# Third layer's attention projections as three rounded products each, with the weights split by ScalarE and VectorE

## The reference, cut to what matters

```
h = modulate(rms_norm_2(x, norm_gain[i, 0]), sh1, sc1)
y = swa_sink_attention(h, swa_w_in[j], swa_qk_gain[j], swa_sinks[j], swa_w_out[j], cos, sin)
x = x + g1 * y
h = modulate(rms_norm_2(x, norm_gain[i, 1]), sh2, sc2)
x = x + g2 * swiglu(h, ffn_w_gate[i], ffn_w_up[i], ffn_w_down[i])
```

## Time and profile before

| | us |
|---|---|
| median of 3 runs (lowest, highest) | 1933.69 (1932.38, 1936.08) |
| the profiled execution's own time | 1934.44 |
| its span | 1932.2 |
| TensorE busy | 1751.9 (91%) |
| VectorE busy | 1185.4 (61%) |
| ScalarE busy | 854.7 (44%) |
| GpSimd busy | 56.8 (3%) |
| mean granted clock of TensorE | 0.972 of full speed |

### The profile page before, as it was taken

The page is one execution under the profiler, slowest core; times in us unless marked ns, Lnnn a source line. Parts: engine busy times, 40 slices in busy tenths (PEclk is TensorE's granted clock), DMA queues, the critical chain, the costliest instruction groups (busy, mean ns, idle before and its releaser), DMA issues.

```text
span 1932.2 us, 32871 instructions
## 1 busy us (share of the span) xinstructions
PE 1751.9 (91%) x13662; PEld 1432.8 (74%) x13662; DVE 1185.4 (61%) x2062; ACT 854.7 (44%) x1531; POOL 56.8 (3%) x96
## 2 busy tenths in 40 slices
PE   7998877677677699999999899999999999999999
PEld 4897544344344489888888798887688888988888
DVE  1885211011010288898877898884888887787674
ACT  2565100000000257655545665643565554766553
POOL 0200000000000000100000000000000000000000
PEclk9999998998998999999999999999999999999999
DMA  9777999999999975678674278775268866334543
GB/s 403 293 281 288 400 428 429 428 429 427 428 428 429 426 306 216 243 286 311 254 283 149 88 283 326 278 275 199 88 262 301 309 248 252 132 132 175 179 160 143
DMA packets 42771, 550.31 MB, mean 285 GB/s; under 512 B 5536, under 2 KB 6048, under 8 KB 8352
## 3 DMA queue, kind: packets, MB, share of 16 engines
q1 hardware_dynamic: 35136, 452.13, 58.9%
q0 software_dynamic: 7520, 96.56, 13.1%
HBM read 547.53 MB, written 1.05 MB: 284 GB/s over the span
## 4 chain that ended last, share of the span: by engine, by line
PE 66%; DMA 23%; DVE 8%; ACT 3%; issue 1%; SPq 0%; ACTq 0%; DVEq 0%
PE bank L709 24%; DMA ada_ring<-in_moe_side 16%; PE bank L713 13%; PE bank L699 12%; DMA ring<-in_moe 3%; PE bank L1136 3%; PE bank L1033 2%; PE bank L684 2%; DMA ring<-in_v 1%; PE bank L1141 1%; DMA ada_ring<-in_ada_last 1%; DVE ring_parts L2514 1%; PE bank L1327 1%; PE bank L805 1%; PE bank L1190 1%
## 5 line engine op out<-in xcount | busy, mean ns | idle before, releaser
L713 PEld LDWEIGHTS bank<-acts,ring_parts 128*128 128x128 f32 x2120 | 299.1, 190 | 23.3
L713 PE MATMUL bank<-acts,ring_parts 128*128 128x256 f32 x2120 | 315.1, 282 | 0.0
L709 PE MATMUL bank<-acts,mixT_parts 128*128 128x512 f32 x1004 | 252.8, 392 | 0.0
L2445 DVE TENSOR_TENSOR mixT<-mixT,bank 128x128 f32<-128x128 f32 x32 | 9.2, 288 | 340.5 <-ACT mixT L1711 340.5
L699 PE MATMUL bank<-acts,ring_parts 128*128 128x256 f32 x728 | 204.9, 281 | 0.0
L709 PEld LDWEIGHTS bank<-acts,mixT_parts 128*128 128x128 f32 x1004 | 180.0, 189 | 31.8
L1502 ACT CAST mixT_parts<-ring 128x1024 fp32r<-128x1024 f32 (+1 forms) x140 | 139.7, 1001 | 82.2 <-PE bank L713 79.5
L709 PE MATMUL bank<-acts,xn_parts 128*128 128x512 f32 x640 | 160.3, 392 | 0.0
L699 PEld LDWEIGHTS bank<-acts,ring_parts 128*128 128x128 f32 x728 | 137.9, 189 | 0.0
L709 PEld LDWEIGHTS bank<-acts,xn_parts 128*128 128x128 f32 x640 | 115.1, 189 | 20.6
L2342 DVE CUSTOM_DVE_ANT_0 ada_ring<-ada_ring,c_row 128x1024 f32<-128x1024 f32 x108 | 127.0, 1220 | 0.0
(11 more groups left out here) (438 smaller groups left out, 3333.8 us busy)
## 6 DMA issues: line engine op xcount, KB each, us to landing
ring<-in_moe SPq DMA_DIRECT2D x48, 2048.0 KB, 27.2
ada_ring<-in_moe_side SPq DMA_DIRECT2D x48, 2048.0 KB, 25.9
ada_ring<-in_ada POOLq DMA_DIRECT2D x45, 2048.0 KB, 9.8
ring<-in_gu SPq DMA_DIRECT2D x44, 2048.0 KB, 8.8
ring<-in_down SPq DMA_DIRECT2D x32, 1408.0 KB, 6.3
ring<-in_qk SPq DMA_DIRECT2D x12, 2048.0 KB, 8.5
ring<-in_out SPq DMA_DIRECT2D x9, 2048.0 KB, 8.4
ring<-in_na SPq DMA_DIRECT2D x8, 2048.0 KB, 8.9
```

Of the source, the lines that this page charges most:

```text
L709: mm(dst[:, :], w, both(*x), start=start, stop=False)
L713: return mm(dst[:, 0:T], w, x[0], start=False, stop=stop)
```

## The change

Layer 2's key, value and query products become split products, and its normalised input is split as in the other layers.

- The four places that asked whether a layer is split no longer ask. `normalise_split` runs for layer 2, with the casts of the first two weight pieces ahead of the norm and the third within it; the weights of keys and values are three pieces (0, 1 keys, 2 values) of one chunk, with high halves in the `piece_hi` buffers.
- TensorE's `swa_keys` takes, for each k tile, both key products (six instructions), each k tile when its low half is there, and then the values, 3 x 8 products of 128 columns for each half of the tokens.
- Each of the eight query tiles is cast by ScalarE (`cast_query`) and subtracted by VectorE (`low_query`). There are two buffers for the high halves, the DFT constants and `gact1`. ScalarE casts tile 0 after the key squares, 1 and 2 within the first steps, and tile j + 2 at the end of its turn j. VectorE subtracts tile 0 first, tile 1 after the cosine part of the keys, and tile j + 1 at the end of its turn j. TensorE waits for the subtraction of tile j ahead of the first half of query j.
- Squares of keys and queries go to `four_sq` instead of `xsq`, which holds the high half of the input now.
- VectorE's wait for the end of the value product moves ahead of the norm of the keys, since `qn` holds a high half until then.
- The counts of the semaphores follow.

```
-                        wait_chunk(pe, n)
-                        w = chunk3(n, 3 * P)
-                        project(bank[0][:, 0:T], w, 0, hT, x0)
-                        project(bank[0][:, T:2 * T], w, P, hT).then_inc(sw["k_proj"], 1)
-                        rows(bank[1][:, 0:T].rearrange("p (t n) -> p t n", t=TT), w, 2 * P, P, hT).then_inc(used[n % RING], 1)
+                        for k in range(KT):
+                            pe.wait_ge(h_lo, split_norms(i, False) + k + 1)
+                            for f in range(2):
+                                if k == 0:
+                                    pe.wait_ge(attn_lo, piece_splits(i) + f + 1)
+                                m = split_product(bank[0][:, f * T:(f + 1) * T], (kv_hi[f][:, k, :], part["w_kv"](n, f)[:, k, :]),
+                                                  (part["xsq"][:, k, :], part["hT"][:, k, :]), k == 0 and f == 0, k == KT - 1, True)
+                        m.then_inc(sw["k_proj"], 1)
+                        pe.wait_ge(attn_lo, piece_splits(i) + 3)
+                        for t in range(TT):
+                            for k in range(KT):
+                                m = split_product(bank[1][:, t * P:(t + 1) * P], tuple(part[x][:, k, t * P:(t + 1) * P] for x in ("xsq", "hT")),
+                                                  (kv_hi[2][:, k, :], part["w_kv"](n, 2)[:, k, :]), k == 0, k == KT - 1)
+                        m.then_inc(used[n % RING], 1)
...
                     def swa_query(j, k0, k1):
 
                         n = FIRST["qs"] + j // 4
-                        if j % 4 == 0 and k0 == 0:
-                            wait_chunk(pe, n)
-                        w = chunk3(n, 512)
+                        if k0 == 0:
+                            pe.wait_ge(attn_lo, piece_splits(i) + 3 + j + 1)
                         for k in range(k0, k1):
-                            m = mm(bank[j % 2][:, 0:T], w[:, k, j % 4 * P:(j % 4 + 1) * P], hT[:, k, :], start=k == 0, stop=k == KT - 1)
+                            m = split_product(bank[j % 2][:, 0:T], (query_hi[j % 2][:, k, :], part["w_gu"](n, j % 4)[:, k, :]),
+                                              (part["xsq"][:, k, :], part["hT"][:, k, :]), k == 0, k == KT - 1)
...
+                def cast_query(j):
+
+                    n = FIRST["qs"] + j // 4
+                    if j % 4 == 0:
+                        wait_chunk(act, n)
+                    if j == 1:
+                        act.wait_ge(sf["qn_ready"], 2 * base + 1)
+                    copy(query_hi[j % 2], full["w_gu"](n, j % 4)).then_inc(attn_hi, 1)
...
+                    cast_query(0)
                     swa_inverse(1, pair_of(bank[2]), xn[:, 0:2, :], xn[:, 2:4, :])
+                    cast_query(1)
                     swa_raw(0)
                     swa_inverse(2, bank[2][:, 0:T], xn[:, 0, :], xn[:, 2, :])
+                    cast_query(2)
                     for j in range(1, PAIRS + 3):
...
+                        if j + 2 < PAIRS:
+                            cast_query(j + 2)
...
+                def low_query(j):
+
+                    dve.wait_ge(attn_hi, piece_splits(i) + 3 + j + 1)
+                    n = FIRST["qs"] + j // 4
+                    V.tensor_tensor(part["w_gu"](n, j % 4), full["w_gu"](n, j % 4), query_hi[j % 2].bitcast(F32), ALU.subtract).then_inc(attn_lo, 1)
+
                 def swa():
+                    low_query(0)
                     dve.wait_ge(sf["rinv"], base + 1)
+                    wait_used(dve, FIRST["kv"])
...
-                    wait_used(dve, FIRST["kv"])
+                    low_query(1)
                     V.tensor_copy(vv[:, 0:2, :], bank[1][:, 0:T].rearrange("p (t n) -> p t n", t=TT)).then_inc(sf["v_ready"], 1)
...
                         if j >= 2:
                             dve.wait_ge(sf["t_done"], base + j - 1)
                             V.tensor_copy(probT_l[:, 1, 0:TRI], bank[7][:, 0:TRI]).then_inc(sf["pt_dve"], 1)
+                        if j + 1 < PAIRS:
+                            low_query(j + 1)
```

More of the change, by code:

```diff
@@ L187, in split_views @@
             v["w_gu"] = lambda n, f: ring[n % RING][:, :].rearrange("p (k n) -> p k n", k=KT)[:, :, f * P:(f + 1) * P]
+            v["w_kv"] = lambda n, f: ring[n % RING][:, 0:KT * 3 * P].rearrange("p (k n) -> p k n", k=KT)[:, :, f * P:(f + 1) * P]
             v["w_piece"] = lambda n, f: ring[n % RING][:, f * KT * P:(f + 1) * KT * P]
@@ L464, in piece_splits, with pieces @@
         def piece_splits(layer):
-            return 3 * NA_PAIRS + 8 + 8 * layer + PIECES * split_before(layer)
+            return 3 * NA_PAIRS + 8 + 8 * layer + sum(pieces(n) for n in range(layer))
+        def pieces(layer):
+            return 3 + PAIRS if KINDS[layer] == "swa" else PIECES
         def out_splits(layer):
-            return piece_splits(layer) + PIECES * (KINDS[layer] in SPLIT)
+            return piece_splits(layer) + pieces(layer)
         def split_norms(layer, ffn):
-            return 2 * KT + 6 + KT * (2 * layer + split_before(layer + ffn))
+            return 2 * KT + 6 + KT * (3 * layer + ffn)
         def piece_chunk(layer, p):
@@ L1332, in swa_square_sum @@
                         pe.wait_ge(sw["squared"], j + 2)
-                        mm(bank[2][:, 0:T], cst("headones"), xsq[:, 0, :], start=True, stop=True).then_inc(sf["ssum"], 1)
+                        mm(bank[2][:, 0:T], cst("headones"), four_sq[:, 0:T], start=True, stop=True).then_inc(sf["ssum"], 1)
                     def swa_rotate(j):
@@ L1735, in cast_piece @@
             def cast_piece(i, p):
+                if KINDS[i] == "swa":
+                    if p == 0:
+                        wait_chunk(act, FIRST["kv"])
+                    copy(kv_hi[p], full["w_kv"](FIRST["kv"], p)).then_inc(attn_hi, 1)
+                    return
                 if p % 4 == 0:
@@ L1765, in early @@
                             cast_piece(i, p)
-                    split_h = KINDS[i] in SPLIT
-                    norm(4 + 2 * i, xT, (x_done, KT * (1 + 2 * i), 1), hT, gcol(0), scol(mods(i), 0), high=split_h or None, early=early if split_h else None,
-                         middle=(lambda: cast_piece(i, 2)) if split_h else None, mods=3 + 2 * i)
+                    norm(4 + 2 * i, xT, (x_done, KT * (1 + 2 * i), 1), hT, gcol(0), scol(mods(i), 0), high=True, early=early,
+                         middle=lambda: cast_piece(i, 2), mods=3 + 2 * i)
                 base = epoch(i)
@@ L2485, in low_piece @@
                 dve.wait_ge(attn_hi, piece_splits(i) + p + 1)
+                if KINDS[i] == "swa":
+                    n = FIRST["kv"]
+                    V.tensor_tensor(part["w_kv"](n, p), full["w_kv"](n, p), kv_hi[p].bitcast(F32), ALU.subtract).then_inc(attn_lo, 1)
+                    return
                 n = piece_chunk(i, p)
@@ L2503, in _ @@
             for i in layers:
-                if KINDS[i] not in SPLIT:
-                    normalise(4 + 2 * i)
-                elif i > 0:
+                if i > 0:
                     normalise_split(4 + 2 * i, split_norms(i, False), 0, mods(i), 0, lambda: low_piece(i, 2))
@@ L2875, in _ @@
                     add_squares(6 + 2 * i, 1, KT - 2)
-                if i + 1 in layers and KINDS[i + 1] in SPLIT:
+                if i + 1 in layers:
                     for p in range(2):
```

8 lines of the change are left out of this document (5 added, 3 removed).

## The result

The changed kernel takes 1962.13 us (median of 3 runs, 1961.04 to 1963.32) where the kernel before takes 1933.69: a ratio of 1.0149, interval 1.0135 to 1.0162. That is 28.4 us slower; the forecast was 23.8 us slower (1957.5, range 1947 to 1966).

A forecast was written before the change was run, and what follows sets the result against it. The prediction took layer 2's loop to be bound by a ring of TensorE and VectorE with little spare. 1934.44 + 14.7 (waits) + 9.0 (clock) + 0.1 (layer start) = 1958.2, set to 1957.5 against the median; range 1947 to 1966 us.

The forecast's parts named there:

- The waits: Layer 2's pair loop: TensorE waits for VectorE's subtraction before queries 2 to 7, 14.7 us in all, product savings included.
- M + 3.77: VectorE's turn in layer 2: the subtraction starts 3.77 us after the start M of the maxima, in the copy's successor's place.
- The clock: TensorE in layer 2's loop: granted clock falls to half after each of six new pauses, 1.5 us each, 9.0 us.
- Rival 2: Layer 2's loop: clock falls for longer than one stretch each time, up to 1975 us, more likely 1965; chance 0.07.
- the prediction's sign: Layer 2's loop: scores 10.1 us apart at full clock, 11 to 12 with the clock falls.
- The start of the layer: Layer 2 up to the scores of pair 0: gains and losses net to 0.1 us, bounds -1.5 and +2.
- Its own signs: Start of layer 2: last down product to scores 0 within 1 us of 27.2; values over 5 us refute 85 ns.
- The nearest rounded product of that width is L1177, two in 0.17 us, 85 ns each: Layer 2's value products: 85 ns per rounded product of 128 columns, so the values cost 0.5 us more.
- the clock half until about 1324: Layer 2's key products: half clock until about 1324, keys ending about 1328.8, so 0.8 to 1.0 us gained.
- 1: Layer 2's loop: the clock does not fall in the new pauses, or falls where it costs nothing; 1948.5 us; chance 0.07.
- rival 3: Layer 2's loop: subtraction ready in time, VectorE's order the bound, 7.46 us a turn, 1932.6 us, no change; chance 0.05.
- Rival 4: Layer 2's loop: subtraction ready, only TensorE's work counts, 5.6 us gained, 1928.1 us; chance 0.03.

The follow-up runs named there:

- e2: Changed kernel with eight unused full-precision products put into each of TensorE's six pauses, behind the sums of squares of queries 1 to 6; 1951.66 us.
- e1: Changed kernel with VectorE's subtraction of query tile j + 1 moved ahead of the maxima of pair j - 1; 1933.09 us.
- e4: On top of e1, the high half of query 1 gets its own buffer, its cast and subtraction ahead of the norm of the keys; 1932.92 us.
- e6: On top of e5, GpSimd instead of VectorE subtracts query tiles 2 to 7, as soon as they are cast; 1936.22 us.
- e7: Changed kernel with the subtraction of query tiles 2 to 7 made twice; 1970.21 us.
- e8: As e3, the same added products but in the order 256, 128, 64 columns; one run, 1979.0 us.
- e5: On top of e4, the values made turned over: weights in the array, 256 tokens moving, then two transposes and a second copy; 1926.59 us.
- e11: The kernel of e5 run again, beside e10; 1928.95 us, ratio 0.9982.
- e3: Changed kernel with 144 unused rounded products after the values, 48 each of 64, 128 and 256 columns in that order; one run, 1982.95 us.
- e10: On top of e5, GpSimd subtracts query tiles 4 to 7, each after the VectorE scaling that stands in its way; 1927.6 us.

## Why the prediction was right, and where its terms were off
The measured 1962.13 lies 4.6 us over the forecast and inside the range. The three terms, 14.7, 9.0 and 0.1, measured 16.8, 10.4 and 2.25 in the trace: each was too low, and the range was wide enough for all three.

**The waits: mechanism right, 14.7 forecast, 16.8 measured.** Moving the subtraction takes them away, doubling it lengthens each by 1.13 to 1.25 us, and TensorE's rows name it as the releaser. The start of the subtraction, M + 3.77 in the forecast, is M + 3.78. The period was to be 10.09 at full clock and is 10.48 in e2. The missing 0.4 lies in the half queries: I took 12 products at 118 ns, 1.42 us, and they take 1.52 up to the rotation and 1.62 up to the scores; the rotation takes 0.53 for 0.43.

**The clock: mechanism right, 9.0 forecast, 10.4 measured.** There were six falls for six pauses, as forecast. Five began within the pause; the fourth began at 1387.7, 1.3 us after its pause had ended, while TensorE worked. Four stretches at half clock lasted 3.1 to 3.4 us and two 6.7:

```profile
1360.50:1367.20 6.70, 5.75 (x24) 4.39 (x25) 2.72 (x9) 1.67 (x5) 0.00 (x0) 0.50 0.00 1
1374.20:1377.40 3.20, 2.85 (x13) 2.85 (x14) 0.30 (x1) 0.71 (x1) 0.00 (x0) 0.50 0.29 123
1387.90:1391.00 3.10, 3.10 (x14) 1.74 (x13) 1.86 (x8) 0.37 (x1) 0.00 (x0) 0.50 0.00 0
```

Rival 2 had longer stretches each time; it came true in two of six. Why those two, the runs leave open. With them the turns are 11.8 to 13.1 us, where the prediction's sign was 11 to 12.

**The start of the layer: wrong, +0.1 forecast, +2.25 measured.** From T0, before to after, it divides into:

| stretch | before | after | difference | forecast |
|---|---|---|---|---|
| to the first value product | 12.64 | 13.07 | +0.4 | -0.8 to -1.0 |
| values | 3.57 | 5.31 | +1.7 | +0.5 |
| sum of the keys' squares and query 0 | 4.31 | 3.73 | -0.6 | -0.6 |
| keys' rotation to the sum of squares of query 0 | 1.81 | 2.98 | +1.2 | +1.2 |
| to scores 0 | 4.87 | 4.36 | -0.5 | -0.3 |

The forecasts in the last column add up to between -0.2 and 0.0; the prediction wrote +0.1. Its own signs were missed here: scores 0 within 1 us of 27.2 (29.45), and the values under 5 us (5.31).

Two steps failed. "The nearest rounded product of that width is L1177, two in 0.17 us, 85 ns each": two products beside a wider one, with 111 ns the pitch in a stream of them. It lies above the figure of the Trainium skill, about 81 ns (TensorE: Matmul & The Clock Gate, Back-to-back issue gap), and near the upper bound of 118 that I had set; it costs 1.2 us more than forecast. And "the clock half until about 1324": in after it stayed at half from 1319.5 to 1326.2. In the executions of e1 and e4 it was half for 3.4 us, and there the first value product comes at T0 + 12.05 and 12.03, 0.6 less than before; so the step nearly holds where the stretch is short, and some 1.0 of the 2.25 us is the longer stretch. It was long in e2, e6, e7 and e8 as well and short in the others, though no edit touches that part of the layer: what decides it, the runs leave open. The row of the rotation is the cast and the subtraction of query 1, rightly priced; e4 takes it away.

**The rivals.** 1 falls by the rows of half clock; e2 is what it would have been, 1951.7 for its 1948.5. 3 and 4 fall for this change, since the subtraction was late in all six turns; but e1 is rival 3 made: it said 7.46 us a turn and no change for a subtraction ready in time, and that gave 7.36 and no change. Rival 4's gain of 5.6 us came in no run by its way: e5 and e11, with one more buffer and the turned values, gained 6.2 and 3.0 us at turns of 7.36.

## What to carry to other kernels
Splitting two tiles ahead is of use only if the last step of the split is ahead too: place each step in its engine's order by the moment its reader needs it, not by where the turn has room. Price a pause of TensorE in a loop at its length and at the clock that may fall with it; here 16.8 us of waits brought 10.4 us of clock with them. Where engines hand work to one another in a ring, taking work off one that is busy for 97% of the turn may give nothing; add up the ring first. And look at the clock in the trace before putting a difference down to an edit: here stretches of half clock of two lengths, in parts no edit touches, moved a layer by 1 us.

## What the runs showed of the hardware that was not expected
**The clock fell without a pause.** In e3 TensorE worked without a break from 1325 on, and the granted clock went from 1.00 to 0.50 at 1339.0, with the last of the 64-column products; it stayed there through those of 128 and came back at 1352.7, while those of 256 ran (columns as in the earlier trace rows):

```profile
1334.00:1338.90 4.90, 4.90 (x47) 4.90 (x45) 0.00 (x0) 0.00 (x0) 0.00 (x0) 1.00 0.00 0
1339.10:1349.00 9.90, 9.90 (x48) 9.90 (x48) 0.00 (x0) 0.00 (x0) 0.00 (x0) 0.50 0.01 2
```

The order of the widths was then turned round, `for width in (T, P, 64)`:

> As e3_widths, 48 extra rounded products at each of three widths, but in the order 256, 128, 64 columns; the same work. Theory N (the granted clock fell in e3_widths because the products were narrow): the products of 256 and of 128 columns run at full clock, 118 and 111 ns each, and the clock falls only during or after those of 64; whole time about 8 us less than e3_widths, 1975. Rival D (it falls some 13 us after the clock last came back, whatever the width): it falls at about the same time, during the products of 128 or 256 columns, and the whole time is within 3 us of e3_widths's 1983.

```profile
1330.50:1341.70 11.20, 11.20 (x101) 11.20 (x99) 0.00 (x0) 0.00 (x0) 0.00 (x0) 1.00 0.01 1
1341.70:1343.40 1.70, 1.70 (x16) 1.70 (x16) 0.00 (x0) 0.00 (x0) 0.00 (x0) 0.93 0.00 0
1343.40:1350.20 6.80, 6.80 (x34) 6.80 (x34) 0.00 (x0) 0.00 (x0) 0.00 (x0) 0.50 0.00 0
```

The products of 256 and 128 columns ran at full clock, and the fall came at 1343.2, among those of 64: 12.7 us after the first added product, for 5.0 in e3. Rival D wanted it some 13 us after the clock last came back; it was 13.7 us in e3 and 20.5 here (from 1322.7), so D falls. In both orders 64-column products were what TensorE worked on when the clock fell, as theory N has it. That is one run of each order, and it does not show the cause. The whole time, 1979.0 where N said 1975 and D at least 1980, decides nothing. The values of after, 48 products of 128 columns, ran at full clock throughout.

**GpSimd's subtraction** of 128x1024 takes 2.36 us (2.46 where VectorE's instruction collides), twice VectorE's 1.22, and on queries 4 to 7 it was as good: e10's layer is as long as e5's.
